# First mixer of a transformer kernel: first weight tile ahead of the parameters, products of zeros at the start, GpSimd's sums behind the context's scaling

## The chip, the cores and the metric

The kernel runs on one core of one Trainium2 chip. The metric is the device time of one execution in microseconds (us). TensorE is called PE below, VectorE DVE, ScalarE ACT, GpSimd POOL, and SyncE, which only issues loads, SP.

## The reference

Two transformer blocks, all in float32, 256 tokens of width 1024. The change touches only the opening of the first block: the modulation vectors, the normed inputs of the 256 tokens (`x`) and of the 256 context tokens (`ctx`), and the projections of both.

```python
mod = jax.nn.silu(c) @ w_mod[i] + b_mod[i]
sh1, sc1, g1, sh2, sc2, g2 = jnp.split(mod[:, None, :], N_MOD, axis=-1)
mod_c = jax.nn.silu(c_ctx) @ w_mod[i] + b_mod[i]
h_lat = modulate(x_lat, norm1_g[i], sh1, sc1)      # rms_norm(x, g) * (1 + scale) + shift
h_ctx = modulate(x_ctx, norm1_g[i], csh1, csc1)
...
q, v, zf, zb, g = jnp.split(h @ w_in, N_HG_PROJ, axis=-1)   # w_in: 1024 x 5120
```

After that come the gated scan of the mixer, a mixture of experts and four further layers. Nothing of them is changed.

## The kernel before

The program of each engine is written out by hand in its own function (`sync_program`, `tensor_program`, `scalar_program`, `vector_program`, `pool_program`). An engine runs its instructions strictly in the order written, and waits on semaphores where it needs another's result. Transposed activations lie as 128 rows by columns of tokens, in two parts (high part and remainder), and every weight tile of 1 MB is loaded by SP into one of three buffers `raw`, cut into a high part `whi` by ACT (`split`, L1292) and a remainder `wlo` by DVE (`split`, L1824), and used by PE in three products. `take()` moves each engine to its next weight tile and splits the tile three further on.

The opening, in the order of PE's `hgrn()`:

1. `columns(0)` transposes the 113 rows of the parameter group 0 (`c`, `c_ctx`, `norm1_g`, ..., `b_mod`, `hg_gnorm`) with the identity `CST`. It waits for `first.all(9)`: nine loads (the identity and eight small ones), all issued by SP ahead of anything else. DVE copies the result to `PRM`; ACT makes `silu(c)` of it (`cs`, L1371) and its high part (L1373), DVE the remainder (L2016).
2. `mod_rows(0)` multiplies these four columns with two tiles of `w_mod` of 1 MB each (`load_first(0)`, L691). In the trace each product of PE is two passes.
3. `rows.all(16)`: PE waits for sixteen loads of parameters of the later layers, which ACT issues as the very first thing in its program (`load_rows(ac, k, rows)`, k from 1 to 4). The last two are `conv_dw_w`, 124 rows of 512 bytes each. Then come four small transposes, `columns(1)` to `columns(4)`.
4. `mod_rows(1)`, the transposes of `x` (`norm("hg_x")`), `mod_cols(0)` and `(1)`, `mod_rows(2)` and `(3)`, `mod_cols(2)` and `(3)`.
5. Four projections q (`proj_b(("q", j))`), weight items 0 to 3. Between the first and the second stand the transposes of the context (`norm("hg_c")`). The fourth uses the PSUM bank of the first, which is free once ACT has taken silu of it (`QO`, L1415).
6. The projections v: weight items 4 to 7, two for each half `c`. Each half uses banks 0 to 3, and the second half can enter bank m only when the first half's result has been copied out of it: banks 0 and 2 by DVE (L2105), 1 and 3 by ACT (L1429).
7. `z` projections and the units of the scan.

Beside this the rest of the modulation (columns 4 to 9 of `w_mod` in tiles of 512) is summed without PE's products. For each c from 4 to 9, SP loads two tiles `MRAW` (`load_mod(2c-8)` and `load_mod(2c-7)`), ACT multiplies each in place by `silu(c)` (`products(n)`, four instructions, L1365), and POOL adds them up (`row_sums(c)`: L2654, L2656, L2659). PE sums over the 128 rows in `mod_sums(c)`, at a place given by the table `MOD_SUMS`. There are four buffers `MRAW`, so that `load_mod(4)` and `(5)` wait until POOL is done with `row_sums(4)`. SP's order is also fixed: `load_mod(4)`, `load_mod(5)`, `load(6)`, `load(7)`, `load_mod(6)`, `load_mod(7)`, `load(8)`, `load_mod(8)`, ... where `load(i)` is weight item i.

The context's scaling is DVE's `modulated(1, q)`: eight instructions (L2031) that write `FTC`. ACT then makes the high part (`norm("hg_c", HC, ...)`, L1317) and DVE the remainder (L2038).

Of the kernel before, what the change touches and what calls it, by code (L numbers as in the profile page):

```python
# [9 lines left out]
ACT = mybir.ActivationFunctionType  # L10
# [4 lines left out]
EPS = 1e-6  # L15
# [98 lines left out]


MOD_FIRST = (0, 2, 1, 3)
MOD_SUMS = ((4,), (5,), (6,), (7,), (8,), (9,))
READ_OUT = {4: 0, 6: 1, 7: 2}


# [94 lines left out]
def build(nc, I, out, table):  # L215

    with ExitStack() as ctx:
# [86 lines left out]
        eps = SM[:, 0:1]  # L304
# [154 lines left out]
        def sync_program(sp):  # L459
# [45 lines left out]
            def load_first(j):  # L505

                for half in range(2):
                    w = I["w_mod"][0][512 * half:512 * half + 512, 512 * MOD_FIRST[j]:512 * MOD_FIRST[j] + 512]
                    sp.dma_start(MFIRST[2 * j + half].rearrange("p (k n) -> p k n", k=4),
                                 w.rearrange("(k p) n -> p k n", p=128)).then_inc(s_modf[2 * j + half], 16)  # L510

            sp.dma_start(CST[:, C_ID:C_ID + 128], I["consts"][:, C_ID:C_ID + 128]).then_inc(*first())
            load_rows(sp, 0, first)
            load_first(0)
            load_first(1)
            for i in range(2):
                sp.dma_start(X[i], I["x"][0, 128 * i:128 * i + 128, :]).then_inc(*xin())
# [57 lines left out]
        def tensor_program(pe):  # L575
# [210 lines left out]
            def spread(p, b):  # L786
# [7 lines left out]
                                      start=True, stop=True)  # L794
                x.then_inc(*mm("hg_spread", p))

            def shifts():

                b = banks.next(pe, RING, "shifts")
                pe.wait_ge(*router.all(3))  # L800
                pe.wait_ge(*vps.at("mod_cols", 7))
                for k in range(8):
                    x = pe.matmul(bank[b][:, 0:16], sh2[:, k:k + 1].to_broadcast([128, 128]), rw[:, k, :], start=k == 0,
                                  stop=k == 7)
                x.then_inc(*mm("shifts"))

            def hgrn():
                pe.wait_ge(*first.all(9))
                columns(0)
                mod_rows(0)  # L810
                pe.wait_ge(*rows.all(16))
                for k in range(1, 5):
                    columns(k)
                mod_rows(1)
                pe.wait_ge(*xin.all(2))
                norm("hg_x", X, late=True)
                rms_rows("hg_x")
                mod_cols(0)
                mod_cols(1)
                mod_rows(2)  # L820
                mod_rows(3)
                mod_cols(2)
                mod_cols(3)
                for j in range(4):
                    proj_b(("q", j), H16, 256, "hg_x" if j == 0 else None)
                    if j == 0:
                        pe.wait_ge(*cin.all(2))
                        norm("hg_c", XC, late=True, apart=SIDE)
                        rms_rows("hg_c")
                pe.wait_ge(*consts.all(1))  # L830
                for n in MOD_SUMS[0]:
                    mod_sums(n)
                pe.wait_ge(*vlo.at("n", "hg_c", 3))
                for c in range(2):
                    for half in range(2):
                        i, w = take()
                        for m in range(4):
                            if half == 0:
                                banks.hold(pe, m, "v", c, m)
                            for k in range(4):  # L840
                                q = 4 * half + k
                                cc = slice(128 * m, 128 * m + 128)
                                x = mm3(bank[m][:, :], H16[0][:, q, cc], H16[1][:, q, cc], w[0][:, k, :], w[1][:, k, :],
                                        q == 0, q == 7)
                        x.then_inc(*prj("item", i))
                        for n in MOD_SUMS[2 * c + half + 1]:
                            mod_sums(n)
                    prj.also("v", c)
                proj_b(("z", 0), H16, 512)
                for n in MOD_SUMS[5]:  # L850
                    mod_sums(n)
                proj_b(("z", 1), H16, 512)
                for u in range(8):
                    p = READ_OUT.get(u)
                    unit_scores(u)
                    unit_state(u)
                    if u == 6:
                        shifts()
                    if u < 6:
                        proj_b(("z", u + 2), H16, 512)  # L860
                    if p is not None:
                        sums(p, 1)
                        proj_b(("g", p), H16)
                    unit_out(u)
                    if p is not None:
                        spread(p, 2)
                proj_b(("g", 3), H16)
                for j in range(4):
                    pe.wait_ge(*vlo.at("hg_y", j))
                    proj_a("hg", Y8, 2 * j, j == 0, j == 3)  # L870
                    if j == 0:
                        sums(3, 4)
                    if j == 1:
                        spread(3, 5)
# [408 lines left out]
        def scalar_program(ac):  # L1283
# [81 lines left out]
                    ac.mul(w[:, k, :], w[:, k, :], cs[:, x, 0:1]).then_inc(*act("products", n))  # L1365

            def hgrn():
                for k in range(1, 5):
                    load_rows(ac, k, rows)
                ac.wait_ge(*vps.at("columns", 0))  # L1370
                ac.activation(SM[:, 2:18], prm("c", 0, 16), ACT.Silu).then_inc(*act("silu"))  # L1371
                ac.wait_ge(*act.last())
                ac.copy(CSv[:, :, 0:2], cs).then_inc(*act("cs"))  # L1373
                def mod_out(j):
                    c = MOD_FIRST[j]
                    ac.wait_ge(*prj.at("mod_rows", c))
                    if j >= 2:
                        ac.wait_ge(*trn.at("mod_cols", MOD_FIRST[j - 2]))
                    b = banks.of("mod_rows", c)
                    ac.copy(MRS[j % 2], bank[b][0:4, :]).then_inc(*act("mod_rows", c))  # L1380
                    banks.free(("mod_rows", c), act)
# [22 lines left out]
                sum_squares(XC, "hg_c", 4)  # L1404
                rstd("hg_c")
                split(2)
                products(0)
                products(1)
                for j in range(4):
                    take()  # L1410
                    if j == 0:
                        norm("hg_c", HC, shifted=True, late=True, ft=FTC)
                    ac.wait_ge(*prj.at("b", ("q", j)))
                    b = banks.of("b", ("q", j), 0)
                    ac.activation(QO[:, 2 * j:2 * j + 2, :], bank[b][:, :], ACT.Silu).then_inc(*aps("q", j))  # L1415
                    banks.free(("b", ("q", j), 0), aps)
                    if j in (0, 3):
                        n = (2, 0, 0, 4)[j]
                        products(n)
                        products(n + 1)  # L1420
                for c in range(2):
                    for half in range(2):
                        take()
# [394 lines left out]
        def vector_program(ve):  # L1818
# [194 lines left out]
            def hgrn():  # L2013
# [94 lines left out]
                ve.wait_ge(*consts.all(1))  # L2108
                for n in MOD_SUMS[5]:
                    mod_cols(n)  # L2110
                for d in range(2):
                    own(ve.memset(SC[d], 0.0))
                unit_vec(0)
                take()

                def routing():

# [495 lines left out]
                take()  # L2613
                add_out("sb")

            own(ve.memset(eps, EPS))
            hgrn()
            moe()
            ret(0)
# [121 lines left out]
```

## Time and profile before

| | us |
|---|---|
| median of 3 runs (lowest, highest) | 2050.31 (2048.95, 2051.76) |
| the profiled execution: its own time | 2049.77 |
| the profiled execution: span from first to last instruction | 2048.4 |
| PE busy over the span | 1945.6 (95%) |
| DVE busy | 1334.5 (65%) |
| ACT busy | 1077.6 (53%) |
| POOL busy | 87.2 (4%) |

Durations come from the profiled execution, whose span leaves 1.37 us of its own time outside. The opening that the change touches ends at about 144 us of the span, where the first `z` projection is done.

### The profile page before, as it was taken

What the parts mean: (1) busy time and instruction counts of PE and PEld (TensorE: products, weight loads), DVE (VectorE), ACT (ScalarE), POOL (GpSimd) and SP (SyncE); (2) the same over time, 40 slices, a digit from 0 to 9 for tenths busy, and PEclk for the clock granted to TensorE, in tenths of its full rate; (3) what the DMA queues carried; (4) which work ended last, traced back from release to release, by engine and by line L of the source; (5) the groups of instructions that cost most, each with busy time, mean ns of one, the idle gap of its engine ahead of it and who ended that gap; (6) DMA issues with size and microseconds to landing.
All of it is one profiled execution on the core that took longest, in us unless ns stands there. A gap on an engine that the chain in (4) does not pass through costs nothing.

```text
span 2048.4 us, 26258 instructions
## 1 busy us (share of the span) xinstructions
PE 1945.6 (95%) x10771; PEld 1643.9 (80%) x10771; DVE 1334.5 (65%) x1667; ACT 1077.6 (53%) x1340; POOL 87.2 (4%) x40
## 2 busy tenths in 40 slices
PE   8899989999989999999988999999999999999997
PEld 3788877778879888888876788797788898888886
DVE  3847765688875566656796656647656675667654
ACT  3756664577754455444544544545544454555442
POOL 0650000000000000000000000000000000000000
PEclk9999999999999999999999999999999999999999
DMA  9761215699945444555421455542355555345552
GB/s 338 253 203 62 70 55 203 219 325 315 321 165 165 145 147 163 193 195 189 150 83 62 145 204 181 184 156 82 105 203 191 179 185 175 122 157 193 178 205 73
DMA packets 230689, 355.37 MB, mean 173 GB/s; under 512 B 7697, under 2 KB 180522, under 8 KB 230314
## 3 DMA queue, kind: packets, MB, share of 16 engines
q1 hardware_dynamic: 230018, 353.47, 50.9%
q8 instruction: 86, 1.41, 0.3%
q10 hardware_dynamic: 552, 0.22, 0.0%
q14 instruction: 33, 0.27, 0.0%
HBM read 352.62 MB, written 1.05 MB: 173 GB/s over the span
## 4 chain that ended last, share of the span: by engine, by line
PE 84%; DVE 9%; ACT 5%; issue 1%; DMA 1%; ACTq 0%; SPq 0%; POOL 0%; DVEq 0%
PE bank L586 13%; PE bank L588 12%; PE bank L587 12%; PE bank L622 12%; PE bank L603 5%; PE bank L620 5%; PE bank L604 5%; PE bank L605 5%; DVE wlo L1824 2%; PE bank L1150 2%; PE bank L691 1%; ACT whi L1292 1%; DVE ARENA L2464 1%; ACT ARENA L1302 1%; PE bank L910 1%
## 5 line engine op out<-in xcount | busy, mean ns | idle before, releaser
L1824 DVE TENSOR_TENSOR wlo<-raw,whi 128x2048 fp32r<-128x2048 f32 x282 | 662.3, 2354 | 250.8 <-ACT whi L1292 250.2
L1292 ACT CAST whi<-raw 128x2048 fp32r<-128x2048 f32 x282 | 536.4, 1907 | 152.3 <-PE bank L588 117.5
L622 PE MATMUL bank<-HH,whi 128*128 128x512 f32 x1024 | 368.3, 400 | 4.7 <-DVE HH L1869 4.7
L586 PE MATMUL bank<-whi,YH 128*128 128x512 f32 x816 | 320.6, 393 | 8.9 <-DVE YL L2508 5.6
L603 PE MATMUL bank<-HH,whi 128*128 128x256 f32 (+1 forms) x1024 | 314.1, 307 | 11.5 <-ACT ARENA L1415 6.0
L588 PE MATMUL bank<-whi,YL 128*128 128x512 f32 x816 | 319.4, 391 | 0.0
L587 PE MATMUL bank<-wlo,YH 128*128 128x512 f32 x816 | 319.3, 391 | 0.0
L604 PE MATMUL bank<-HL,whi 128*128 128x256 f32 (+1 forms) x1024 | 306.6, 299 | 0.0
L605 PE MATMUL bank<-HH,wlo 128*128 128x256 f32 (+1 forms) x1024 | 306.4, 299 | 0.0
L620 PE MATMUL bank<-HH,wlo 128*128 128x256 f32 x896 | 252.6, 282 | 0.0
L622 PEld LDWEIGHTS bank<-HH,whi 128*128 128x128 f32 x1024 | 193.7, 189 | 48.8 <-issue 3.7
L603 PEld LDWEIGHTS bank<-HH,whi 128*128 128x128 f32 x1024 | 198.8, 194 | 20.9 <-ACT ARENA L1415 6.2
L604 PEld LDWEIGHTS bank<-HL,whi 128*128 128x128 f32 x1024 | 198.9, 194 | 6.7 <-issue 1.9
L605 PEld LDWEIGHTS bank<-HH,wlo 128*128 128x128 f32 x1024 | 198.8, 194 | 5.1
L586 PEld LDWEIGHTS bank<-whi,YH 128*128 128x128 f32 x816 | 153.7, 188 | 41.8 <-DVE YL L2508 6.0
L587 PEld LDWEIGHTS bank<-wlo,YH 128*128 128x128 f32 x816 | 153.6, 188 | 33.2
L588 PEld LDWEIGHTS bank<-whi,YL 128*128 128x128 f32 x816 | 153.5, 188 | 32.9
L620 PEld LDWEIGHTS bank<-HH,wlo 128*128 128x128 f32 x896 | 170.6, 190 | 2.8
L586 PE MATMUL bank<-whi,HH 128*128 128x512 f32 x384 | 154.3, 402 | 4.8 <-issue 2.5
L1597 ACT COPY ARENA<-bank 128x256 f32<-128x256 f32 x128 | 41.3, 375 | 211.4 <-PE bank L622 211.4
L588 PE MATMUL bank<-whi,HL 128*128 128x512 f32 x384 | 150.6, 392 | 0.0
L587 PE MATMUL bank<-wlo,HH 128*128 128x512 f32 x384 | 150.3, 391 | 0.0
(376 smaller groups left out, 2253.6 us busy)
## 6 DMA issues: line engine op xcount, KB each, us to landing
raw<-in_ffn_w SPq DMA_DIRECT2D x128, 1024.0 KB, 5.3
raw<-in_ret_w_in SPq DMA_DIRECT2D x48, 1024.0 KB, 5.1
ARENA<-in_w_mod SPq DMA_DIRECT2D x21, 1024.0 KB, 8.1
raw<-in_hg_w_in SPq DMA_DIRECT2D x20, 1024.0 KB, 9.9
raw<-in_ret_w_out SPq DMA_DIRECT2D x16, 1024.0 KB, 4.9
raw<-in_moe_w_gate SPq DMA_DIRECT2D x26, 512.0 KB, 4.9
raw<-in_moe_w_up SPq DMA_DIRECT2D x26, 512.0 KB, 6.4
raw<-in_moe_w_down SPq DMA_DIRECT2D x12, 1024.0 KB, 7.8
```

The source lines that it names most:

```text
L586: pe.matmul(ps, lh, rh, start=start, stop=False)
L587: pe.matmul(ps, lh, rl, start=False, stop=False)
L588: return pe.matmul(ps, ll, rh, start=False, stop=stop)
L603: pe.matmul(ps, w[0][:, k, c], ah, start=begin, stop=False, skip_group_check=True)
L604: pe.matmul(ps, w[0][:, k, c], al, start=False, stop=False, skip_group_check=True)
L605: x = pe.matmul(ps, w[1][:, k, c], ah, start=False, stop=k == 7, skip_group_check=True)
L620: pe.matmul(bank[bs[m]][:, 0:256], w[1][:, k, c], HW[:, k, 0:256], start=False, stop=False, skip_group_check=True)
L622: x = pe.matmul(bank[bs[m]][:, :], w[0][:, k, c], HW[:, k, :], start=k == 0, stop=k == 7, skip_group_check=True)
L1150: x = pe.matmul(bank[bf][:, c:c + 256], DG[:, n % NDG, :], HP[:, f, w:w + 256], start=w == (9 if f == 5 else 0), stop=w == 30)
L1292: ac.copy(whi[i % NS][:, :], raw[place[i]][:, :]).then_inc(*whi_("w", i))
L1597: ac.copy(TL[j % 2][:, m, :], bank[b][:, 256:512]).then_inc(*aps("low", st, j))
L1824: ve.tensor_tensor(wlo[i % NS][:, :], raw[place[i]][:, :], f32(whi[i % NS][:, :]), SUB).then_inc(*wlv("w", i))
```

## The change

SP loads the two tiles of `mod_rows(0)` first; the identity comes behind them, and the eight small loads of parameter group 0 move from SP to ACT. ACT's sixteen loads of the other parameters move behind `silu(c)` and its high part, and ACT applies silu once to a column of zeros before them. DVE clears `HXX` at the start, and PE multiplies these zeros six times (256 columns each) ahead of `columns(0)` and twice behind it. On ACT `products(0)` and `products(1)`, on which `row_sums(4)` waits, move behind silu of the first q projection, `products(1)` also behind the context's high part; `products(2)` and `(3)` move from the first to the third q projection. Every `mod_sums` moves one place later.

```diff
-MOD_SUMS = ((4,), (5,), (6,), (7,), (8,), (9,))
+MOD_SUMS = ((), (4,), (5,), (6,), (7,), (8,), (9,))
...
+            load_first(0)
             sp.dma_start(CST[:, C_ID:C_ID + 128], I["consts"][:, C_ID:C_ID + 128]).then_inc(*first())
-            load_rows(sp, 0, first)
-            load_first(0)
             load_first(1)
...
+            def warm(count):
+
+                b = banks.next(pe, RING, "warm", count)
+                pe.wait_ge(*vec.at("zeros"))
+                for _ in range(count):
+                    x = pe.matmul(bank[b][:, 0:256], HXX[:, 0:128], HXX[:, 0:256], start=True, stop=True)
+                x.then_inc(*mm("warm", count))
+                banks.free(("warm", count), mm)
...
             def hgrn():
+                warm(6)
                 pe.wait_ge(*first.all(9))
                 columns(0)
+                warm(2)
                 mod_rows(0)
                 pe.wait_ge(*rows.all(16))
...
                 proj_b(("z", 1), H16, 512)
+                for n in MOD_SUMS[6]:
+                    mod_sums(n)
...
             def hgrn():
-                for k in range(1, 5):
-                    load_rows(ac, k, rows)
+                load_rows(ac, 0, first)
+                ac.wait_ge(*vec.at("zeros"))
+                ac.activation(SM[:, 2:3], HXX[:, 0:1], ACT.Silu).then_inc(*act())
                 ac.wait_ge(*vps.at("columns", 0))
+                ac.wait_ge(*act.last())
                 ac.activation(SM[:, 2:18], prm("c", 0, 16), ACT.Silu).then_inc(*act("silu"))
                 ac.wait_ge(*act.last())
                 ac.copy(CSv[:, :, 0:2], cs).then_inc(*act("cs"))
+                for k in range(1, 5):
+                    load_rows(ac, k, rows)
...
                 split(2)
-                products(0)
-                products(1)
                 for j in range(4):
                     take()
-                    if j == 0:
-                        norm("hg_c", HC, shifted=True, late=True, ft=FTC)
                     ac.wait_ge(*prj.at("b", ("q", j)))
                     b = banks.of("b", ("q", j), 0)
                     ac.activation(QO[:, 2 * j:2 * j + 2, :], bank[b][:, :], ACT.Silu).then_inc(*aps("q", j))
                     banks.free(("b", ("q", j), 0), aps)
-                    if j in (0, 3):
-                        n = (2, 0, 0, 4)[j]
-                        products(n)
-                        products(n + 1)
+                    if j == 0:
+                        products(0)
+                        norm("hg_c", HC, shifted=True, late=True, ft=FTC)
+                        products(1)
+                    if j == 2:
+                        products(2)
+                        products(3)
+                products(4)
+                products(5)
...
+                ve.wait_ge(*pmod.at("sums", 9))
                 for d in range(2):
                     own(ve.memset(SC[d], 0.0))
                 unit_vec(0)
                 take()
+                for n in MOD_SUMS[6]:
+                    mod_cols(n)
...
-            own(ve.memset(eps, EPS))
+            ve.memset(eps, EPS).then_inc(*vec())
+            own(ve.memset(HXX, 0.0))
+            vec.also("zeros")
```

SP's queue at the start, as it was (L453 and L451 are the small parameters, L509 the tiles of `w_mod`):

```order
L512 DMA CST<-in_consts 128x128
L453 DMA ARENA<-in_c 8x128
L451 DMA ARENA<-in_c_ctx 8x128
L453 DMA ARENA<-in_norm_g 8x128 x2
L453 DMA ARENA<-in_hg_lb_fwd 16x128
L453 DMA ARENA<-in_hg_lb_bwd 16x128
L453 DMA ARENA<-in_b_mod 48x128
L453 DMA ARENA<-in_hg_gnorm 1x128
L509 DMA raw<-in_w_mod 128x4x512 x3
```

and as it is now:

```order
L509 DMA raw<-in_w_mod 128x4x512 x2
L513 DMA CST<-in_consts 128x128
L509 DMA raw<-in_w_mod 128x4x512
L509 DMA ARENA<-in_w_mod 128x4x512
L516 DMA X<-in_x 128x1024 x2
```

The identity now stands third, behind 2 MB of weights, and the small parameters are gone from this queue.

ACT at the start, now (before, the sixteen loads that begin with `in_norm_mix` stood first, and `L1371 ACT_TABLE_LOAD` behind them; L1382 is silu of zeros, L1385 silu of `c`, L1387 its high part, L1405 the exponential for the gates' bounds):

```order
L453 DMA ARENA<-in_b_mod 48x128
L453 DMA ARENA<-in_hg_gnorm 1x128
L1382 ACT_TABLE_LOAD
L1382 ACTIVATE SM<-ARENA 128x1
L1385 ACTIVATE SM<-PRM 128x16
L1387 CAST CS<-SM 128x8x2
L453 DMA ARENA<-in_norm_mix 32x128
L453 DMA ARENA<-in_norm_ffn 32x128
...
L449 DMA ARENA<-in_sb_k_norm 1x64
L446 DMA ARENA<-in_conv_dw_w 124x128 x2
L1405 ACT_TABLE_LOAD
```

The sixteen loads moved from the head of ACT's program to behind the high part of `silu(c)`.

ACT around the q projections, as it was (L1292 cuts a weight tile, L1365 are the products, L1317 the context's high part, L1415 silu of q):

```order
L1310 ACTIVATE SM<-SM 128x2
L1292 CAST whi<-raw 128x2048
L1365 ACTIVATE ARENA<-ARENA,SM 128x512 x8
L1292 CAST whi<-raw 128x2048
L1317 CAST HH<-ARENA 128x2x256 x4
L1415 ACT_TABLE_LOAD
L1415 ACTIVATE ARENA<-bank 128x512
L1365 ACTIVATE ARENA<-ARENA,SM 128x512 x8
L1292 CAST whi<-raw 128x2048
L1415 ACTIVATE ARENA<-bank 128x512
```

and as it is now (the same instructions at L1304, L1377, L1329 and L1427):

```order
L1322 ACTIVATE SM<-SM 128x2
L1304 CAST whi<-raw 128x2048 x2
L1427 ACT_TABLE_LOAD
L1427 ACTIVATE ARENA<-bank 128x512
L1377 ACTIVATE ARENA<-ARENA,SM 128x512 x4
L1329 CAST HH<-ARENA 128x2x256 x4
L1377 ACTIVATE ARENA<-ARENA,SM 128x512 x4
L1304 CAST whi<-raw 128x2048
L1427 ACTIVATE ARENA<-bank 128x512
L1304 CAST whi<-raw 128x2048
L1427 ACTIVATE ARENA<-bank 128x512
L1377 ACTIVATE ARENA<-ARENA,SM 128x512 x8
```

The first eight products are cut in two and stand behind silu of q, and the next eight two weight tiles later.

## Rows read from the trace of the kernel before

**Rows 1.** Windows: us, busy time of PE, PEld, DVE, ACT, POOL, granted clock, DMA, GB/s.

```profile
60.00:80.00 20.00, 13.96 (x91) 13.20 (x89) 15.33 (x14) 13.49 (x18) 10.48 (x4) 0.83 0.78 265
```

**Rows 2.** Chain that ended last, first 200 us: start, duration, what.

```profile
9.66 9.73 PE bank L691 x16
```

**Rows 3.** Timeline of the first 20 us: start, duration, engine, line [idle before].

```profile
0.74 0.42 ACTq L453 DMA_DIRECT2D ARENA<-in_norm_mix  x1
4.28 1.50 SPq L509 DMA_DIRECT2D raw<-in_w_mod  x3
5.45 0.45 PE L654 MATMUL bank<-CST,ARENA 113*128 113x113 f32 x1 [5.45 <-DMA ARENA<-in_hg_gnorm]
6.59 0.78 ACTq L446 DMA_DIRECT2D ARENA<-in_conv_dw_w  x2
8.94 0.21 ACT L1373 CAST CS<-SM 128x16 fp32r<-128x16 f32 x1
19.31 0.36 PEld L654 LDWEIGHTS bank<-CST,ARENA 104*128 104x128 f32 x4 [0.86 <-DMA ARENA<-in_conv_dw_w]
```

**Rows 4.** DMA issues, windows 4.2:4.5 and 4.6:5: KB each, median us to landing.

```profile
raw<-in_w_mod SPq DMA_DIRECT2D x1, 1024.0 KB, 5.2
...
raw<-in_w_mod SPq DMA_DIRECT2D x2, 1024.0 KB, 6.5
```

**Rows 5.** Queue q10 (ACT's), windows 7.5:10 and 10:18.25; q1 (SP's), 18.25:20: packets, MB, share.

```profile
q10 hardware_dynamic: 20, 0.00, 0.9%
...
q10 hardware_dynamic: 260, 0.13, 5.7%
...
q1 hardware_dynamic: 229, 0.70, 102.3%
```

**Rows 6.** Windows of L691 alone, PE and PEld, two stretches of `mod_rows(0)`.

```profile
9.66:15.00 5.34, 5.34 (x7) 0.85 (x8) 1.00 1.06 374
15.10:19.00 3.90, 3.90 (x10) 0.70 (x8) 1.00 1.06 376
```

**Rows 7.** Windows of all engines around PE's two idle stretches.

```profile
70.90:76.00 5.10, 5.08 (x24) 5.08 (x25) 2.01 (x4) 5.10 (x9) 0.10 (x1) 0.50 1.03 368
79.40:82.70 3.30, 0.86 (x3) 0.04 (x1) 3.30 (x2) 3.30 (x5) 3.22 (x2) 1.00 0.00 0
83.40:86.70 3.30, 3.30 (x10) 2.52 (x9) 3.30 (x1) 3.30 (x6) 3.22 (x2) 0.50 0.88 269
```

**Rows 8.** L2031 alone, windows 33:47 (tokens) and 58:68.5 (context): ns min/median/max.

```profile
L2031 DVE TENSOR_SCALAR ARENA<-ARENA,SM x8: 403/406/413, 33.7 to 46.8; 128x256 f32<-128x256 f32 x8
...
L2031 DVE TENSOR_SCALAR ARENA<-ARENA,SM x8: 399/402/4682, 58.2 to 67.9; 128x256 f32<-128x256 f32 x8
```

**Rows 9.** Timelines of POOL, SP and PE, 58 to 100 us.

```profile
58.11 4.62 POOL L2654 TENSOR_TENSOR ARENA<-ARENA 128x2048 f32<-128x2048 f32 x1 [8.84 <-ACT ARENA L1365]
66.57 0.93 SPq L499 DMA_DIRECT2D ARENA<-in_w_mod  x2
70.92 0.58 PE L603 MATMUL bank<-HH,whi 128*128 128x256 f32 x1 [6.04 <-ACT ARENA L1415]
88.28 6.54 POOL L2654 TENSOR_TENSOR ARENA<-ARENA 128x2048 f32<-128x2048 f32 x1
100.69 4.61 POOL L2654 TENSOR_TENSOR ARENA<-ARENA 128x2048 f32<-128x2048 f32 x1
```

**Rows 10.** DMA issues, window 89:90: one tile of `w_mod`, weight item 8.

```profile
ARENA<-in_w_mod SPq DMA_DIRECT2D x1, 1024.0 KB, 7.5
raw<-in_hg_w_in SPq DMA_DIRECT2D x1, 1024.0 KB, 9.9
```

**Rows 11.** Timeline where the second half of v begins.

```profile
108.57 2.56 ACT L1365 ACTIVATE ARENA<-ARENA,SM 128x512 f32<-128x512 f32 x4 [0.17 <-DMA ARENA<-in_w_mod]
109.03 0.47 PE L586 MATMUL bank<-whi,HH 128*128 128x512 f32 x1 [0.94 <-DVE ARENA L2105]
111.04 1.05 ACT L1429 COPY ARENA<-bank 128x512 f32<-128x512 f32 x2
```

## The prediction, made before the run

> **What bounds the opening now.** I read the chain of waits first, then the timeline of each engine, then the DMA queues. In the chain PE's products with `w_mod` run from 9.66 to 19.39 us without another engine between [rows 2]: up to there PE is the chain. Two things slow it. It starts only at 9.66, because the parameters land at 5.45 and the silu chain takes the rest (high part of `silu(c)` at 8.94) [rows 3]; and its passes are slow at first: 7 begin in 5.34 us (0.76 each), later 10 in 3.90 us (0.39) [rows 6]. Right behind stands PE's wait for the last of ACT's sixteen loads, which ends at 19.31 [rows 3].
>
> From 60 to 80 us PE is busy 13.96 of 20 us at a granted clock of 0.83 [rows 1]. The cause is DVE's scaling of the context. The same eight-fold instruction takes 0.40 us at its median, but two or three of its eight wait out POOL's sums, the longest 4.68 us, and the eight last from 58.2 until 68.3 [rows 8]. POOL's first sum starts at 58.11 [rows 9]. Silu of the first q stands behind all this on ACT, holds the bank of the fourth q, and PE idles 6.04 us until 70.92 [rows 9]. Then it runs 5.1 us at clock 0.50, the 1.2 GHz level [rows 7].
>
> **Part 1, the start.** The first tile of `w_mod` landed 5.2 us after its issue at 4.28, the next two at a median of 6.5 us, so the second about 7.8 us after 4.79, at 12.6 [rows 3, 4]. Issued from 0.75 they should land at about 6.0 and 9.0. But the identity is now behind these 2 MB in SP's queue: about 9.3. `columns(0)` therefore starts at 9.3 instead of 5.45. Behind it stand the transpose itself, DVE's copy, silu, the high part and the remainder, small operations of which the high part takes 0.21 us [rows 3]; with the gaps between engines I estimate 1.9 us for the five. `mod_rows(0)` starts near 11.2, 1.5 later than before, and `warm(2)` (four passes of half the columns, at most half of 0.76 us each) fits into that gap. Before, its sixteen passes took from 9.66 to the wait at 19.31, less its 0.86 [rows 3], or 8.8 us, 2 to 3 of them lost at the slow pace [rows 6]; now 6.5 without that loss: the end lies at 18 to 20.5, before at 18.5. By itself this is worth between -1 and +1.5 us.
>
> It doesn't decide, since the loads behind it do. ACT now issues its sixteen loads when `silu(c)` is through, at about 10.6. Before, they took from 0.74 to 7.37, or 0.41 each [rows 3], so the last is issued at 17.2. What they meet is a full queue of SP: the DMA share is 1.06 in both windows of 9.66 to 19 [rows 6]. How long small loads take beside such a stream the trace shows: `conv_dw_w` was issued at 6.59 to 7.37, only 20 packets of ACT's queue moved from 7.5 to 10, then 260 from 10 to 18.25, and none after [rows 5]. That is 3.4 us until the first packet and 8 us for the two loads, landed 10.9 us after the last issue. The stream from SP still has over half of its first 12 MB to go at 17 us (374 to 376 GB/s [rows 6]), so I take the same: 17.2 + 10.9 = 28.1. The bounds: no lag at all and half of the 8 us (the last load alone) gives 17.2 + 4 = 21.2; a lag that grows over sixteen loads as it did over the last (2.9 us to 3.4) gives 31. PE stands in `rows.all(16)` until then: `columns(1)` moves from 19.31 to 28.4, **+9.1 us** (+2 to +12). Nothing hides it, because `mod_rows(1)` and everything behind it is queued on PE after this wait. SP's stream stops later as well, as `load_mod(0)` waits for `mod_rows(2)`, so the later loads move along instead of running ahead.
>
> The clock: after the idle 6 us PE ran 5.1 us and more at 0.50, and after a gap of 2.5 us it fell too and ran 3.3 us at 0.50 [rows 7]. Half of such a stretch is lost, 1.7 to 2.8 us. After nine idle us I add **+2.3**.
>
> A rule speaks against this term. The Trainium skill, "DMA: Bandwidth & Descriptors", section "Anatomy of one DMA", gives a load a fixed 2 us (fitted on loads from GpSimd's path) plus its bytes over the bandwidth; an estimate by it is a landing at 19.3 and no wait. The trace disagrees: 10.9 us. The same page, section "Queues, rings and completion order", says that each DMA engine takes turns between queues packet by packet, with which the steady trickle agrees.
>
> **Part 2, the context's scaling.** All times here are on the clock of before; part 1 moves them together. DVE begins the eight instructions at 58.3. `row_sums(4)` can now start only behind `products(1)`: ACT cuts items 2 and 3 (to 55.1), takes silu of q (57.0), does `products(0)` (59.5), the four high parts (62.0) and `products(1)` (64.5); four product instructions take 2.56 [rows 11]. So the scaling runs alone, 8 times 0.34, and ends at 61.0 instead of 68.3. The bank of the fourth q is free at 57, its remainder is cut at 63.3, and PE goes on without a gap: the fourth q ends at 70.5 instead of 79.2. That is 8.7 us won at this point.
>
> Who pays: `row_sums(4)` starts at 64.5 instead of 58.11 and takes at least its 8.4 us (58.11 to 66.57 [rows 9]), end about 73. SP's `load_mod(4)` waits for it (before: 66.57 [rows 9]), and `load(6)` stands behind that on SP. It is issued at about 74 and, by the like pair, lands 9.9 us later [rows 10], at 84. ACT, which has cut items 4 and 5 and done `products(3)` by 74.5, stands before item 6 until 84, and does `products(4)` and `(5)` only after it: to 91.5. `row_sums(6)` starts then; before it started at 88.28 and the next at 100.69 [rows 9]. One sum took 8.4 us without DVE's weight cuts and 12.4 with them (88.28 to 100.69): it ends at 100 to 104. `load_mod(8)` and `(9)` wait for that, and `products(9)`, which before ended at 111.13 [rows 11], 10.4 later than that sum, ends at 110.3 to 114.3. Behind `products(9)` on ACT stands the copy of banks 1 and 3 of the first half of v (before 111.04 [rows 11]), and PE cannot enter bank 1 of the second half without it. PE is there at 97: v's first half runs 71.5 to 93.5, the first bank of the second 2.7 us more. It waits some 16 us. So the 8.7 us won turn into a wait, and what counts is the copy: **+2** (-1 to +3; I take the upper half, since DVE cuts items 6 and 7 just then). Then the clock, as above: **+2.3**, where before PE had a gap of 0.94 us only [rows 11].
>
> The rest I cost at nothing. `mod_sums(9)` is the same eight small products, one place later. DVE's new wait for the last sum is over before the first z projection is (about 11 us after v), and ACT waited for it before. Clearing `HXX` and silu of zeros run in the first 6 us, beside the loads. If that cover were gone they would cost under 2 us together.
>
> **Sum.** 2049.8 (the profiled execution, 0.5 under the median) + 9.1 + 2.3 + 2.0 + 2.3 = 2065.5 us, 0.75% slower.
>
> **The rivals.**
> - Only the scaling's gain passes through: the loads are late (+11.4), but ACT's copy isn't behind (-8.7). Against it stands the order on ACT, copies after `products(9)`; for it, that `load(6)` may land sooner. 2052.5 us. Chance 0.13.
> - The sixteen loads land in time (the fixed cost by the rule above, or 3.4 us of lag alone: 17.2 + 3.4 = 20.6) and v waits: -0.5 to +1.5 and +4.3: 2054.5 us. Chance 0.12.
> - Faster, the other side: SP's stream starts 3.5 us earlier, and so has less left when ACT's loads are issued; the packets of `conv_dw_w` pass beside it without the 8 us, PE goes from `mod_rows(0)` on without a gap, and the 8.7 us of the scaling are kept because the second half of v finds its bank free. It decides from the point where `rows.all(16)` ends before 20.5 and the copy before 103. 2049.8 - 8.7 + 0.5 = 2041.5. Chance 0.12.
> - The forecast: 0.63.
>
> Within 0.2% (4.1 us, about what a measurement of this kernel can tell from no change) lie the first rival and nearly half of the second: same 0.2. Faster 0.14, slower 0.66. The forecast's own range is 2058 (a landing at 21.2 with its cold stretch, then +4) to 2072. To leave no more than 2 in 10 out, the range reaches down over the second and first rival to 2051.
>
> **What would show it.** In the profile after: the first transpose of parameters at 9 to 10 us with the identity as releaser; PE idle from about 19 to 28 before L653's four small transposes, released by `in_conv_dw_w`, and granted clock 0.5 behind it; the eight scalings at 0.4 us each without a long one; no gap before the fourth q; ACT idle about 9 us before it cuts item 6; a gap of PE of some 15 us inside v, released by ACT's copy. The prediction is wrong if the wait before the small transposes is under 3 us, or if the copy comes before PE reaches the second half of v.

## The result and the profile after

The changed kernel takes 2065.22 us (median of 4 runs, 2064.06 to 2068.30), the kernel before 2051.03 (4 runs, 2048.95 to 2052.08). The ratio is 1.0073, with a 95% interval of 1.0061 to 1.0085. Its profiled execution took 2065.97 us, at a span of 2064.7.

The start, in PE's timeline of the changed kernel (start, duration, engine, line; in brackets the idle time before and what ended it). L690 is the line L691 of before, and L653 is L654:

```profile
9.28 0.45 PE L653 MATMUL bank<-CST,ARENA 113*128 113x113 f32 x1 [3.03 <-DMA ARENA<-in_hg_gnorm]
...
11.39 7.42 PE L690 MATMUL bank<-raw,CS 128*4 128x512 f32 x16
...
27.20 0.97 PE L653 MATMUL bank<-CST,ARENA 104*128 104x104 f32 x4 [8.39 <-DMA ARENA<-in_conv_dw_w]
28.10 5.86 PE L690 MATMUL bank<-raw,CS 128*4 128x512 f32 x8
33.79 3.60 PE L690 MATMUL bank<-ARENA,CS 128*4 128x512 f32 x8
```

PE now stands 8.39 us before ACT's sixteen loads. In the kernel before it didn't stand there at all. The transposes followed the last pass of `mod_rows(0)`, which ran to 19.39 [rows 2], without idle time of PE. The 0.86 us of [rows 3] are in the line of the weight loads (PEld), and the last kernel of experiment 5 has the same 0.86 although the sixteen loads had landed long before. The line of the kernel before, then the one of that kernel:

```profile
19.32 0.59 PE L654 MATMUL bank<-CST,ARENA 104*128 104x104 f32 x4
```

```profile
23.99 0.36 PEld L657 LDWEIGHTS bank<-CST,ARENA 104*128 104x128 f32 x4 [0.86 <-issue]
```

Behind the wait of the changed kernel eight passes take 5.86 us, the next eight 3.60, so the clock was low again. The last row of `mod_rows` comes 10.6 us later than before. ACT issued its last two loads here:

```profile
15.51 0.67 ACTq L446 DMA_DIRECT2D ARENA<-in_conv_dw_w  x2
```

From 16.18, the end of these two issues, to PE's release at 27.20 is 11.0 us. The last packets of ACT's queue move by 26.6, 10.4 us after the last issue; before, it was 10.9 [rows 5].

Then the context's scaling (L2031 before, L2048 here), in the timelines of DVE, POOL and SP:

```profile
68.73 2.66 DVE L2048 TENSOR_SCALAR ARENA<-ARENA,SM 128x256 f32<-128x256 f32 x8
...
77.11 9.96 DVE L1841 TENSOR_TENSOR wlo<-raw,whi 128x2048 fp32r<-128x2048 f32 x2 [1.10 <-ACT whi L1304]
```

```profile
75.36 5.15 POOL L2676 TENSOR_TENSOR ARENA<-ARENA 128x2048 f32<-128x2048 f32 x1 [15.55 <-ACT ARENA L1377]
80.59 4.33 POOL L2678 TENSOR_TENSOR ARENA<-ARENA 128x1024 f32<-128x1024 f32 x1
84.99 3.23 POOL L2681 TENSOR_TENSOR ARENA<-ARENA 128x512 f32<-128x512 f32 x1
```

```profile
88.25 0.93 SPq L499 DMA_DIRECT2D ARENA<-in_w_mod  x2
89.22 1.27 SPq L483 DMA_DIRECT2D raw<-in_hg_w_in  x2
```

The scaling is free of POOL: 2.66 us for all eight, where it took 10 us [rows 8]. But POOL's first sum takes 12.9 us instead of the 8.4 of [rows 9], because DVE now cuts items 4 and 5 beside it, and these two cuts take 9.96 us in turn. SP issues item 6 (the lower of its two lines, L483) behind that sum. What hangs on it, from the timelines of ACT, DVE and PE:

```profile
98.93 1.91 ACT L1304 CAST whi<-raw 128x2048 fp32r<-128x2048 f32 x1 [14.18 <-DMA raw<-in_hg_w_in]
...
128.94 1.04 ACT L1446 COPY ARENA<-bank 128x512 f32<-128x512 f32 x2
```

```profile
114.75 2.65 DVE L1841 TENSOR_TENSOR wlo<-raw,whi 128x2048 fp32r<-128x2048 f32 x1 [1.11 <-ACT whi L1304]
117.33 0.67 DVE L1955 TENSOR_TENSOR G1B<-G1B,bank 128x512 f32<-128x512 f32 x1
117.92 1.27 DVE L2122 COPY ARENA<-bank 128x512 f32<-128x512 f32 x2
```

```profile
118.75 0.77 PE L585 MATMUL bank<-whi,HH 128*128 128x512 f32 x1 [12.04 <-DVE ARENA L2122]
129.56 0.80 PE L585 MATMUL bank<-whi,HH 128*128 128x512 f32 x1 [5.35 <-ACT ARENA L1446]
```

The idle time of [rows 9], 6.04 us ahead of the fourth q, is gone. In its place PE idles 17.4 us in two pieces where the second half of v begins; before it idled 0.94 there [rows 11]. The windows behind (PE, PEld, DVE, ACT, POOL, granted clock, DMA share, GB/s) show PE slow for another while:

```profile
120.00:130.00 10.00, 4.65 (x11) 3.19 (x11) 0.00 (x0) 6.08 (x11) 7.57 (x4) 0.67 1.03 359
130.00:140.00 10.00, 10.00 (x35) 7.96 (x35) 4.09 (x1) 6.91 (x9) 8.10 (x2) 0.75 1.08 369
```

The first `z` projection is done 20.4 us later than before (164.26 instead of 143.85 us, the start of ACT's first sigmoid of it). The span is only 16.3 us longer, so 4 us come back behind the mixer, where nothing was changed.

### The profile page after: what moved, and what is told of

Its sections match the earlier page's. It is cut to its first block, busy times and chain, and to the rows that moved or that the text cites. A ratio compares the mean times of both kernels' runs of the same rounds, so it can differ in the third digit from the quotient of the medians.

```text
span 2064.7 us, 26294 instructions
## 1 busy us (share of the span) xinstructions
PE 1952.4 (95%) x10787; PEld 1647.7 (80%) x10787; DVE 1319.3 (64%) x1668; ACT 1076.8 (52%) x1341; POOL 84.9 (4%) x40
## 4 chain that ended last, share of the span: by engine, by line
PE 82%; DVE 8%; ACT 5%; DMA 2%; issue 1%; POOL 1%; ACTq 0%; SPq 0%; DVEq 0%; POOLq 0%
PE bank L585 12%; PE bank L587 12%; PE bank L586 12%; PE bank L621 12%; PE bank L602 5%; PE bank L619 5%; PE bank L604 5%; PE bank L603 5%; DVE wlo L1841 2%; PE bank L1162 2%; ACT whi L1304 1%; DVE ARENA L2484 1%; PE bank L690 1%; ACT ARENA L1314 1%; DMA raw<-in_hg_w_in 1%
## 5 line engine op out<-in xcount | busy, mean ns | idle before, releaser
L1841 DVE TENSOR_TENSOR wlo<-raw,whi 128x2048 fp32r<-128x2048 f32 x282 | 654.8, 2327 | 266.8 <-ACT whi L1304 266.3
L1304 ACT CAST whi<-raw 128x2048 fp32r<-128x2048 f32 x282 | 536.3, 1907 | 158.6 <-PE bank L587 119.2
L585 PE MATMUL bank<-whi,HH 128*128 128x512 f32 x384 | 155.9, 406 | 20.5 <-DVE ARENA L2122 12.0
```

Source lines behind the costliest of these rows:

```text
L585: pe.matmul(ps, lh, rh, start=start, stop=False)
L1304: ac.copy(whi[i % NS][:, :], raw[place[i]][:, :]).then_inc(*whi_("w", i))
L1841: ve.tensor_tensor(wlo[i % NS][:, :], raw[place[i]][:, :], f32(whi[i % NS][:, :]), SUB).then_inc(*wlv("w", i))
```

## The experiments

Expectations call the kernel before "the kernel before" and the changed kernel by that name; "mod_rows' end" is the end of `mod_rows(3)`. All shifts are against the profiled execution of before. The kernel before was timed again beside the experiments, with medians of 2050.57, 2049.86 and 2050.62 us, so that times of different experiments can be compared to about 1 us.

**1. Each part alone.** The first kernel has the changed start (`sync_program`, the zeros, ACT's loads) and ACT's and PE's order of before from the first projection on.

```diff
-                    if j == 0:
-                        products(0)
-                        norm("hg_c", HC, shifted=True, late=True, ft=FTC)
-                        products(1)
+                products(0)          # ahead of the q loop, as before
+                products(1)
...
-MOD_SUMS = ((), (4,), (5,), (6,), (7,), (8,), (9,))
+MOD_SUMS = ((4,), (5,), (6,), (7,), (8,), (9,), ())
```

> Only the start is changed (first weight tiles ahead, parameters on ScalarE, sixteen loads behind silu, products of zeros); GpSimd's sums stand where they stood before. Theory (late loads): PE waits about 8 us for the sixteen loads and runs cold after, the first q projection starts 10.6 us later than before as in the changed kernel, total +10.6: about 2061.5 us. Rival (all of the slowdown is in the sums, the late start is hidden by the loads of the weights): within 2 us of before.

Measured: 2056.89 us (2055.75 to 2057.96), before 2050.57, ratio 1.0030 (1.0021 to 1.0040). The wait came as expected, the time is 4.6 us under the expected one. In its timeline of PE the wait for the sixteen loads and the two later gaps are

```profile
27.39 0.97 PE L653 MATMUL bank<-CST,ARENA 104*128 104x104 f32 x4 [6.88 <-DMA ARENA<-in_conv_dw_w]
...
81.48 0.58 PE L602 MATMUL bank<-HH,whi 128*128 128x256 f32 x1 [6.04 <-ACT ARENA L1431]
...
119.61 0.47 PE L585 MATMUL bank<-whi,HH 128*128 128x512 f32 x1 [0.94 <-DVE ARENA L2121]
```

The 6.04 and the 0.94 us of before are both there again, 10.6 us later: the start shifts the opening as a whole, and the gaps inside v belong to the other part. That part alone, with the start of before (the diff above the other way round):

> Only the sums are moved behind the context's scaling; the start is that of before. Theory (the sums hold up weight item 6 and the copies of v): the scaling takes 2.7 us instead of 10, the fourth q ends 8.7 us earlier, and PE then waits over 15 us inside v; z starts 4 to 10 us later than before, total +4 to +10: about 2057 us. Rival (the scaling's gain passes through, all of the loss is at the start): -8.7, about 2042 us.

Measured: 2062.19 us (2059.87 to 2062.51), ratio 1.0050 (1.0033 to 1.0067). That is 11.6 us over its before, where 4 to 10 were expected. PE's two gaps are there with the start of before:

```profile
110.34 0.76 PE L586 MATMUL bank<-whi,HH 128*128 128x512 f32 x1 [10.46 <-DVE ARENA L2108]
...
121.30 0.79 PE L586 MATMUL bank<-whi,HH 128*128 128x512 f32 x1 [5.50 <-ACT ARENA L1432]
```

By these medians the second part is the dearer one, 11.6 us against 6.3, although the scaling itself is 7.4 us shorter. Alone they sum to 17.9, together they cost 14.2; at `z` it is 10.8 and 11.9 against 20.4. So of the start's 10.8 us at `z` only 6.3 are left in the times, while the sums keep 11.6 of 11.9: what comes back behind the mixer goes with the changed start.

**2. Which wait costs the start its time.** The changed kernel, with `columns(1)` to `(4)` later:

```diff
-                pe.wait_ge(*rows.all(16))
-                for k in range(1, 5):
-                    columns(k)
                 mod_rows(1)
+                pe.wait_ge(*rows.all(16))
+                for k in range(1, 5):
+                    columns(k)
```

> The changed kernel, but PE waits for the sixteen loads and makes their four transposes behind the second pair of w_mod products instead of ahead of it. Theory (only the place of the wait costs): the loads land at 27.2 us as they did, PE fills 6.9 us of the wait with products at the high clock, waits about 1.5 us, and everything behind is 8 to 9 us earlier than in the changed kernel: about 2056.5 us. Rival (the weight stream from SP is what is late, not these loads): the second pair of products waits for its own tiles, no gain over 2 us.

Measured: 2055.37 us (2054.51 to 2057.64), ratio 1.0024 (1.0014 to 1.0034), so 9.9 us below the changed kernel. PE's timeline:

```profile
10.95 11.81 PE L690 MATMUL bank<-raw,CS 128*4 128x512 f32 x24
22.60 3.60 PE L690 MATMUL bank<-ARENA,CS 128*4 128x512 f32 x8
...
27.25 0.59 PE L653 MATMUL bank<-CST,ARENA 104*128 104x104 f32 x4 [1.06 <-DMA ARENA<-in_conv_dw_w]
```

The loads land where they did (27.2), but PE has work until 26.2 us, and mod_rows' end is only 1.25 us later than before. PE's two waits inside v are still there (11.92 and 6.13 us), and `z` is 9.7 us later than before. The wait and the cold passes behind it are nearly the whole cost of the start.

**3. What sets these loads.** Two kernels, one execution each. First the identity ahead of the 2 MB of `w_mod` in SP's queue:

```diff
-            load_first(0)
             sp.dma_start(CST[:, C_ID:C_ID + 128], I["consts"][:, C_ID:C_ID + 128]).then_inc(*first())
+            load_first(0)
```

> The changed kernel, with SP's load of the identity ahead of the first w_mod tile instead of behind it, all else as changed. Theory (the identity, behind 1 MB on SP's queue, ends the first wait of columns(0), at 9.28 us in the changed kernel): columns(0) starts at 7.5 to 8 us, mod_rows(0) 1 to 1.5 us earlier than its 11.39, with the last pass of mod_rows(0) no earlier than the tiles of w_mod allow. Rival (ACT's own parameter loads end it, since their queue still had packets until 8.9 us): columns(0) at 9.0 to 9.3 us. Either way the wait for the sixteen later loads of ACT stays until 26 to 28 us, since ACT issues them behind its SiLU and they land 11 us after the last issue; so mod_rows' end moves by under 1.5 us.

```profile
8.81 0.32 PE L653 MATMUL bank<-CST,ARENA 113*128 113x113 f32 x1 [2.32 <-DMA ARENA<-in_hg_gnorm]
...
26.54 0.97 PE L653 MATMUL bank<-CST,ARENA 104*128 104x104 f32 x4 [7.92 <-DMA ARENA<-in_conv_dw_w]
```

Between the two, nearer the rival: `columns(0)` moves by 0.47 us only. What is left to hold it at 8.8 us are ACT's own eight loads: the last was issued by 4.50 us, and their packets move until about 8.4. No run takes them away, so this is argued and not shown. Mod_rows' end came 1.8 us earlier and the time was 2063.65 us (one run; before 2050.62).

Then the sixteen loads of the changed kernel, issued ahead of ACT's silu:

```diff
                 load_rows(ac, 0, first)
+                for k in range(1, 5):
+                    load_rows(ac, k, rows)
...
-                for k in range(1, 5):
-                    load_rows(ac, k, rows)
```

> The changed kernel, with ACT's sixteen loads for columns(1) to (4) issued right behind its parameter loads, ahead of the table load and the SiLU (4.6 to 10.4 us instead of 10.4 to 16.2). Theory (they land some 11 us after ACT's last issue, wherever that stands): columns(1) starts at about 21.5 us instead of 27.2, the SiLU and with it mod_rows(0) come 1 to 2 us later (12.5 to 13.5 instead of 11.4), and mod_rows ends 5 to 6 us earlier than in the changed kernel. Rival (they land when the SP queue's w_mod traffic lets them, not by their issue): columns(1) stays at 26 to 28 us.

```profile
9.53 0.67 ACTq L446 DMA_DIRECT2D ARENA<-in_conv_dw_w  x2
```

```profile
12.55 9.63 PE L690 MATMUL bank<-raw,CS 128*4 128x512 f32 x16 [1.78 <-DVE CS L2033]
22.42 0.59 PE L653 MATMUL bank<-CST,ARENA 104*128 104x104 f32 x4 [0.24 <-DMA ARENA<-in_conv_dw_w]
```

The theory holds; the first line is ACT's issue of the last two loads, the others are PE's. Issued 6.0 us earlier, released 4.8 us earlier, 12.2 us after the last issue. Mod_rows' end comes 7.4 us before the changed kernel's and the time is 2058.46 us, 6.8 less (one run).

**4. What sets the copy.** The changed kernel, with SP's weight items 6 and 7 ahead of the two `w_mod` tiles that wait for POOL's first sum:

```diff
-                if i in (6, 8, 9, 10):
-                    n = 4 if i == 6 else 2 * i - 10
+                if i == 8:
+                    load_mod(4)
+                    load_mod(5)
+                if i in (8, 9, 10):
+                    n = 2 * i - 10
                     load_mod(n)
```

> The changed kernel, but SP issues weight items 6 and 7 ahead of the modulation tiles that wait for GpSimd's first sum. Theory (item 6 stands behind that sum): ScalarE's wait of 14.2 us before it cuts item 6 goes, products 4 and 5 end 7 us earlier (they wait for their own tiles then), and so do the third sum and the copies of v: 6 to 8 us less than the changed kernel, about 2058 us. Rival (the chain of sums alone is the bound, item 6 only happens to be late beside it): no gain over 2 us.

Measured: 2055.76 us (2054.03 to 2057.01), ratio 1.0023 (1.0013 to 1.0032), so 9.5 us below the changed kernel. ACT's 14.18 us are gone, `z` is 10.0 us later than before instead of 20.4, but PE still stands before v's second half. The timelines of PE and of DVE:

```profile
117.15 0.76 PE L588 MATMUL bank<-whi,HH 128*128 128x512 f32 x1 [10.54 <-DVE ARENA L2125]
```

```profile
111.31 4.50 DVE L1844 TENSOR_TENSOR wlo<-raw,whi 128x2048 fp32r<-128x2048 f32 x1 [5.27 <-ACT whi L1307]
115.73 0.68 DVE L1958 TENSOR_TENSOR G1B<-G1B,bank 128x512 f32<-128x512 f32 x1
116.33 1.28 DVE L2125 COPY ARENA<-bank 128x512 f32<-128x512 f32 x2
```

It is DVE's copy that PE waits for, and it stands behind DVE's cut of item 8 and `mod_cols(5)`. So the next kernel has in addition the copies of v's first half ahead of item 8 on both engines:

```diff
-                        take()
+                        if c or not half:
+                            take()
...
                         banks.free(("v", c, m), aps)
+                    if c == 0:
+                        take()
+                        products(8)
+                        products(9)
```

> The changed kernel with items 6 and 7 issued first on SP, as in the experiment before, and with both copies of v's first half (ScalarE's and VectorE's) ahead of weight item 8 and of products 8 and 9. Theory (PE's idle time inside v is the wait for those copies): the second half of v starts at about 106 to 109 us, 10 us earlier than with items 6 and 7 alone; total about 2048 us. Rival (the chain of GpSimd's sums binds what follows v, since silu of z waits for the last sum): 2054 us or more, z's silu waits for GpSimd.

Measured: 2049.02 us (2046.29 to 2051.21), before 2049.86, ratio 0.9994 (0.9985 to 1.0004). PE has no gap over 0.3 us from the second weight of v to the first `z`, and is as far there as the kernel before, although it started 10 us later. The rival has a part too: ACT waits there for POOL's last sum, and PE then idles 3.79 us for ACT's sigmoid:

```profile
142.45 1.28 ACT L1350 ACT_TABLE_LOAD   x1 [8.29 <-POOL G2B L2694]
```

**5. The better parts together.** The start of before with POOL's sums behind the scaling, item 6 and the copies as in 4:

> The start of before, with the sums behind the context's scaling, items 6 and 7 first on SP and the copies of v first. Theory: the whole gain of the scaling comes through, 8 to 10 us less than before: about 2041 us. Rival (some other wait takes the gain's place): within 4 us of before, at 2047 or more.

Measured: 2040.59 us (2040.22 to 2044.65), ratio 0.9955 (0.9941 to 0.9968). It is faster than both kernels; `z` comes 8.3 us earlier than before, near the 8.7 us that the scaling had been forecast to win. Then the same with products of zeros ahead of and behind `columns(0)`, in before's order of loads:

```diff
             def hgrn():
+                warm(4)
                 pe.wait_ge(*first.all(9))
                 columns(0)
+                warm(8)
                 mod_rows(0)
```

> The same, with products of zeros in the start of before: four ahead of the first transpose, and eight behind it instead of two, so that PE is busy up to the products with w_mod. Theory (only an unbroken stream keeps the clock at its high level): the first passes of w_mod start at the high clock and take 6.9 us instead of 9.1, 2 to 2.5 us less: about 2039 us. Rival (zeros don't raise the clock, or it falls again all the same): no difference to the kernel without them.

Measured: 2040.00 us (2039.46 to 2041.02), ratio 0.9952 (0.9938 to 0.9965): no difference from the kernel without them that could be told, where 2 to 2.5 us were expected. Yet the zeros did what they are for:

```profile
10.16 7.03 PE L694 MATMUL bank<-raw,CS 128*4 128x512 f32 x16
18.44 0.59 PE L657 MATMUL bank<-CST,ARENA 104*128 104x104 f32 x4 [1.24 <-DMA ARENA<-in_conv_dw_w]
```

Sixteen passes take 7.03 us, against 9.73 in [rows 2] and 8.77 to 9.02 in the three other traces with the start of before, but the sixteen loads are there only at 18.4. Hence one more, with `columns(1)` to `(4)` behind `mod_rows(1)` as in 2:

> e10_with_warm, with the wait for ACT's sixteen loads and columns(1) to (4) behind mod_rows(1) instead of ahead of it. Theory: the zeros' products did raise the clock there (mod_rows(0) took 7.03 us in e10 against 9.73 in the kernel before), and what they gave was given back to the wait for the sixteen loads (1.24 us) and the two short ones around it; with the wait moved, mod_rows ends 1.0 to 1.5 us earlier than in e10 and so does the rest: 2038.7 us (2037.5 to 2040). Rival: something behind mod_rows (the scaling's vectors, POOL's sums) sets the pace, and the time stays at 2040 us, with mod_rows' end still earlier.

Measured: 2039.52 us (2038.58 to 2042.54), ratio 0.9950 (0.9936 to 0.9964). Mod_rows' end moved by 0.5 us, not by 1.0 to 1.5, because the norm of `x` now waits twice for DVE (0.24 and 0.32 us) where it had waited for nothing. The two times can't be told apart.

**6. The kernel before once more,** for a second trace:

> The kernel before, unchanged, for a second profile of it. Theory: the 4 us that the changed kernels win back behind the first mixer, at about 350, 815 and 1050 to 1110 us, come from the place of the chip's low-clock stretches, which differ from one execution to the next: this profile shows some of them gone against the first profile. Rival: they are a property of the kernel, and this profile agrees with the first within 0.5 us everywhere.

Measured: 2050.96 us, span 2049.6. What it shows stands in the next section.

## Why the prediction came out as it did

The forecast was 2065.5 us and the time is 2065.22. The places and the mechanisms were those forecast; of the sizes one was too small by some 5 us, and a saving of 4 us that the forecast had no term for made up for it. That the two came out alike is luck.

- **Start of `columns(0)`: right in time, not in cause.** 9.28 us, forecast 9.3. The prediction put it down to the identity behind 2 MB; experiment 3 shows that this is worth 0.47 us. The eight small loads on ACT's queue are what is left as the cause.
- **`mod_rows(0)` at 11.2, end by itself within -1 and +1.5: right.** 11.39 us, and PE waits from 18.81. Two numbers behind it were wrong. The passes' time "from 9.66 to the wait at 19.31, less its 0.86 [rows 3], or 8.8 us" takes off idle time that PE didn't have; the passes took 9.73 us and ended at 19.39. And "now 6.5 without that loss" was not reached: it took 7.42 us, and 8.98 and 8.90 in experiments 1 and 4 with the same start.
- **The sixteen loads, +9.1: right, a little large.** Measured +7.9 (27.20 against 19.31). The 10.9 us from the last issue held (10.4, and 11.0 to PE's release); the loads were issued in 5.8 us instead of 6.6. Experiments 2 and 3 confirm that the wait costs what it lasts, and that the landing follows the issue. The Trainium skill ("DMA: Bandwidth & Descriptors", "Anatomy of one DMA — SWDGE (gpsimd) path") gives a load on GpSimd's path a fixed 2 us; an estimate by it is a landing at 18.2, ahead of 18.81, and no wait. The trace disagrees: 11.0 us here, and 4.3 from ACT's last small load to PE's release in experiment 3 (4.50 to 8.81).
- **Cold clock, +2.3: right.** The eight passes behind the wait took 5.86 us against 3.60 for the next eight, 2.3 us. With the wait the start costs 10.6 us (11.3 against the second trace of the kernel before), forecast 11.4.
- **The scaling, 8.7 us won at that point: right.** 2.66 us, no gap ahead of the fourth q. It was won and lost again, as forecast.
- **The copy of v's first half, +2 (-1 to +3): the term that was mis-sized.** ACT's copy started at 128.94 us; less the 10.6 of the start this is 7.3 us later than the 111.04 of [rows 11]. The step that failed is "`row_sums(4)` starts at 64.5 [...] and takes at least its 8.4 us [...], end about 73". It started 0.3 us and ended 4.6 us later than that (75.36 and 88.22, less the 10.6, are 64.8 and 77.6; in the kernel with the start of before it ran from 67.49 to 79.78), because DVE's cuts of items 4 and 5 stand beside it. The prediction had the price of this in its own text, 12.4 us with the cuts, and used it for the third sum only. Everything behind moved along: item 6, `products(4)` and `(5)`, the third sum (106.37 to 118.52), `products(9)`.
- **A wait was missed.** PE's first gap, 12.04 us, is ended by DVE's copy (L2122), which the prediction didn't name. Experiment 4 shows that it holds PE on its own: with item 6 in time PE still lost 10.54 us to it, and only the second edit took the gap away (2055.76 to 2049.02, 6.7 us, or 6.0 with each against its own before).
- **Cold clock there, +2.3: right.** Between the copy (17.9 us later than before) and `z` (20.4) lie 2.5 us.
- **"The rest I cost at nothing": not right in the trace, nearly so in the time.** Up to `z` the cost is 20.4 us, against 15.7 in the sum. Then 4.1 come back. Two places account for most of it, and experiment 6 shows what one of them is. From 800 to 820 us the profiled execution of before ran at a lower granted clock, the second one (same kernel) didn't. Windows of the two, in this order:

```profile
800.00:820.00 20.00, 18.25 (x95) 15.51 (x94) 13.63 (x24) 11.97 (x21) 2.55 (x2) 0.91 0.38 128
```

```profile
800.00:820.00 20.00, 18.06 (x102) 15.07 (x101) 15.25 (x24) 12.16 (x21) 2.58 (x2) 1.00 0.52 182
```

The second gains 1.5 us on the first there, and so do the changed kernel and all other traces: this is an accident of the profile that the shifts are measured against. The other place is PE's wait for ACT ahead of the router, in the timelines of the kernel before, of its second trace, and of the changed kernel:

```profile
353.29 3.61 PE L1011 MATMUL bank<-ARENA,RWB 128*16 128x256 f32 x16 [2.10 <-ACT ARENA L1524]
```

```profile
354.96 5.12 PE L1011 MATMUL bank<-ARENA,RWB 128*16 128x256 f32 x16 [2.60 <-ACT ARENA L1524]
```

```profile
372.68 3.61 PE L1023 MATMUL bank<-ARENA,RWB 128*16 128x256 f32 x16 [0.77 <-ACT ARENA L1541]
```

It is 1.3 us shorter in the changed kernel. In the seven traces with the changed start, experiment 1's first kernel among them, it lasts 0.69 to 1.42 us; in the four with the start of before and no zeros 2.09 to 2.60, the sums alone (2.37) among them (with zeros ahead of and behind `columns(0)`, in experiment 5, it is 0.91 and 1.04, for DVE). In before's second trace the sixteen passes behind it are slow too, 5.12 us. So the theory of experiment 6 holds at 800 us and not here. Against that trace the changed kernel is 19.5 us behind at `z` and 15.1 at the end; 3.4 of the 4.4 that come back do so at the router. So this saving goes with the changed start. How a start 350 us earlier shortens that wait is open, and so is how much of the 4 us is saved in every execution; the medians, 14.2 apart with 20.4 at `z`, and those of experiment 1 speak for most of it. The forecast had no term for it: without it the time would have been near 2069.

The rivals: the sixteen loads did not land in time (experiment 3 says why), and the gain of the scaling did not pass through; that rival's own condition, ACT's copy not being behind, is what experiments 4 and 5 made true, and then it did pass. "Faster" needed the wait to end by 20.5 and the copy to come by 103: they came at 27.2 and 128.9 (118.3 on the clock of before).

## What to carry to other kernels

Small loads issued beside a full stream from another queue were there only 11 to 12 us after the last issue, in every kernel here in which PE waited for them, so they belong ahead of the stream, or their consumer behind the longest work that doesn't need them; moving one wait past `mod_rows(1)` was worth 9.9 us here, where the whole change cost 14.2. When work is moved on one engine, list for each neighbour what its shifted work now runs beside, and price it with the row that has that company: POOL's sum costs 8.4 us alone and 12.9 beside DVE's cuts. And a gain ahead of a fixed order turns into a wait unless what frees the next buffer moves too: 2.66 us of scaling instead of 10 made the kernel slower, until weight item 6 and the two engines' copies stood ahead of the work that waits for POOL; with that, and the start of before, it became 0.45% faster than the kernel before.

## What the runs showed of the hardware

- **POOL and DVE stretch each other.** Alone, POOL's pass over 1024 elements takes 2.37 us and DVE's cut 2.29; side by side 4.33 and 9.96 for two. The Trainium skill ("SBUF — State Buffer", "SBUF: two separate sides") says that the two share a port pair, that the one that starts first holds it for the whole instruction, and that this concerns DVE operations with two SBUF inputs as well. The trace agrees: POOL's 4.33 is near the sum of one of each (2.37 and 2.29, 4.66).
- **Products of zeros raise the clock only for what follows without idle time.** In the first microseconds the column of the granted clock says 1.00 in all kernels, also for passes at half the pace ([rows 6], both windows), so the pace has to be read there. The zeros' passes (256 columns each) take 0.43 us each at first and about 0.2 at the end, so the clock rose during them. After 3.03 us of idle time it was at its lower level (1.2 GHz) for `columns(0)` and the four passes behind it, and up again for nearly all of `mod_rows(0)`:

```profile
1.50:5.40 3.90, 3.90 (x9) 3.19 (x10) 0.00 (x0) 0.79 (x1) 0.00 (x0) 1.00 0.89 288
5.40:6.20 0.80, 0.80 (x4) 0.39 (x3) 0.00 (x0) 0.69 (x2) 0.00 (x0) 1.00 1.05 403
...
9.30:11.40 2.10, 2.10 (x6) 1.27 (x7) 0.77 (x5) 0.42 (x2) 0.00 (x0) 0.50 1.05 386
11.50:18.80 7.30, 7.30 (x16) 1.23 (x14) 0.88 (x5) 1.50 (x2) 0.00 (x0) 0.95 1.05 385
```

  These 7.42 us are the best of the traces with this start: experiments 1 and 4 had 8.98 and 8.90 (8.02 in the second kernel of 4), and experiment 3, with 1.78 us of idle time just ahead, 9.63. The four traces with the start of before had 8.77 to 9.73. Only with zeros behind `columns(0)` too, and no idle time, did all sixteen run at full pace, 7.03 us. What that won the sixteen loads took back: PE was released at 18.44, and at 18.66 in the same kernel without zeros.
- **Two executions of one kernel differ by 1 to 3 us in the middle.** The second trace of before is 3.3 us behind the first at 500 us and 1.9 at 1000, with both times within 1.2 us of each other. A shift of a microsecond between two profiles, away from the change, is no evidence of it.
